# Storing the turned blocks of the first expert table in another order: four stores by groups of 32 partitions instead of four by groups of columns

## Chip, cores and metric

The kernel runs on one core of one Trainium2 chip. The metric is the device time of one execution in microseconds. Three runs of the kernel before are shown with their median.

## What is computed

The reference is one layer of a hybrid encoder on 528 positions (16 learned tokens and 512 of the input) of width 2048, in float32:

```python
h += (sigmoid(g_a) * mlstm_branch(...) + sigmoid(g_b) * conv_branch(...)) @ w_o
h += peer(rmsnorm(h), w_q, sub_keys, expert_u, expert_v)      # 8 heads, top 16 of 128 x 128 experts
# in peer, for each token t and each of its 128 chosen experts e:
z   = einsum('thed,td->the', expert_u[eidx], tb)
act = gates * gelu(z)
out = einsum('the,thed->td', act, expert_v[eidx])
```

`expert_u` and `expert_v` are tables of 16384 rows of 2048 floats (128 MB each).

## The kernel before, in words

**Stages.** All large products go through one stream of weight blocks of 128x2048 floats (1 MB): 48 blocks for the mLSTM heads (6 a head, 8 heads), 64 for the convolution branch and the gates (4 to each of 16 channel tiles), 16 each for the mLSTM output, the convolution output, `w_o` and the query projection, and then 128 for the first expert table and 128 for the second. SP loads a block into one of two buffers `w_raw` (line 393), ScalarE makes its rounded part `w_hi` (line 1047), VectorE the rest `w_lo` (line 1424), and TensorE multiplies three times per block of 128 rows of depth (lines 757 to 759): high by high, high by low, low by high. In the first two stages the blocks have either 2x264 moving columns (96 matmuls) or 512 (48 matmuls).

**Two ways through the expert tables.** 384 of the 512 tokens meet the experts densely: all 16384 products by matmul. The last 128 tokens, one to each partition, gather the rows of their 128 chosen experts one after another with an indirect DMA (`u_row`, line 687, for the first table; line 716 for the second), and VectorE takes the dot product. For that the tables must lie in DRAM by rows. The second is copied from DRAM to DRAM (`row_copy`, line 389, 128 copies of 1 MB in runs of 1 KB). The first lies in blocks `u_blocks[m]` of 128 depths x 2048 and must be turned on the way.

**The turned blocks.** For each block m of 128 SP loads 1 MB into one of two buffers `u_raw` (`u_load`, line 396). VectorE turns it with a transpose of 32x32 squares into one buffer `u_turned` (`u_turn`, lines 1426 to 1432). Before it may write there, all four stores of block m-1 must have landed (`u_stored`, line 1434, four semaphores `ur_st`). Then SP, which waits for the turn (line 400), stores the buffer to `u_rows` with four DMAs (line 402) and issues the load of block m+2 (line 405). One turned row of an expert lies in `u_rows` as four pieces of 512 floats, one from each group `a` of 32 partitions. Each of the four DMAs takes a quarter `b` of the columns of all 128 partitions:

```python
for b in range(QD):                                     # QD = 4
    sp.dma_start(u_rows[m, b, :, :, :].rearrange("r a n -> a r n"),
                 bufs[1][:, b * D // QD:(b + 1) * D // QD]).then_inc(ur_st[b], 16)
```

so that its DRAM side has the shape (4, 32, 512) and its SBUF side (128, 512).

**Order of the work.** It is written out by hand. In SP's program each weight load is followed by the stores of one turned block, the load of a further one and, in part of the stages, one or two row copies. In VectorE's program the turns stand between the `w_lo` of successive blocks and the stage's own work (attention of a head; 31 taps of the convolution, line 1616; the merge and the residual, lines 1727, 1730). The turns are spread so: blocks 0 to 37 over the heads, 38 to 98 over the convolution tiles, 99 to 113 over the convolution output, 114 to 127 over `w_o` and the first query blocks, each set with buffers of its own (names with a, b and c). Except at the seams there is one turn to a weight block. The stage of the mLSTM output has one turned block at its start and two row copies to each weight block.

**Who needs `u_rows`.** GpSimd waits for all stores (line 698) after the routing. VectorE computes the row indices of the gather once, ahead of it (lines 1910 to 1918): `ix_z = 128 j + i`, since the row of expert (i, j) is row `(j b r)` of `u_rows` with i = 32 b + r.

Of the kernel before, what the change touches and what calls it, by code (L numbers as in the profile page):

```python
# [33 lines left out]
F32 = mybir.dt.float32  # L34
F32R = mybir.dt.float32r
U32 = mybir.dt.uint32
ALU = mybir.AluOpType
# [4 lines left out]
P = 128  # L42
D = 2048
KT = D // P
# [7 lines left out]
KEYS = 128  # L52
# [19 lines left out]
VSLOT = 3  # L72
V_FIRST, V_LAST = 1, 119
QD = P // 32
# [15 lines left out]
def encoder_block(nc, xT, w_proj, w_gate, b_gate, w_mo, w_co, w_o, w_q, u_blocks, v_blocks, cols,  # L90
# [5 lines left out]
    z_dram = nc.dram_tensor("z_scratch", (NB_E, P, NT), F32, kind="Internal").ap()  # L96
    g_dram = nc.dram_tensor("g_scratch", (NT // CH, P, KEYS * CH), F32, kind="Internal").ap()
    v_rows = nc.dram_tensor("v_rows", (KEYS // GJ, P, GJ, GJ, 256), F32, kind="Internal").ap()
    u_rows = nc.dram_tensor("u_rows", (KEYS, QD, 32, QD, KT * 32), F32, kind="Internal").ap()

    at = [(nc.sbuf_base + 31) // 32 * 32]

# [118 lines left out]
    GB, UG = [GB0, GB1], [UG0, UG1, UG2]  # L221
# [17 lines left out]
    with ExitStack() as ctx:  # L239
# [5 lines left out]
        def sem(name):  # L245
            return ctx.enter_context(nc.semaphore(name))
# [81 lines left out]
        ur_st = [sem(f"u_rows_stored{b}") for b in range(QD)]  # L328
# [39 lines left out]
        def _(sp):  # L368
# [26 lines left out]
            def u_load(m, bufs):  # L395
                sp.dma_start(bufs[0][m % 2][:, :], u_blocks[m]).then_inc(ur_ld[m % 2], 16)

            def u_turned(m, bufs, end):

                sp.wait_ge(ur_turn, m + 1)  # L400
                for b in range(QD):
                    sp.dma_start(u_rows[m, b, :, :, :].rearrange("r a n -> a r n"), bufs[1][:, b * D // QD:(b + 1) * D // QD]  # L402
                                 ).then_inc(ur_st[b], 16)
                if m + 2 < end:
                    u_load(m + 2, bufs)

            for n in range(2, NB_A1 + NB_A2):
                weights(w_proj, n, A1)
                x = n - 2
                if x == U_A1_X - 1:  # L410
                    sp.wait_ge(x_lo, KT)
                    sp.wait_ge(g_rdy, 1)
                    for v in range(2):
                        u_load(U_A1 + v, u_a1)
                if U_A1_X <= x < U_A1_X + U_A2 - U_A1:
                    u_turned(x - U_A1_X + U_A1, u_a1, U_A2)
                if x == U_A2_X - 1:
                    sp.wait_ge(hs_done, 2 * NH)
                    for v in range(2):
                        u_load(U_A2 + v, u_a2)  # L420
                if U_A2_X <= x:
                    u_turned(x - U_A2_X + U_A2, u_a2, U_B2)
                if n < 8:
                    row_copy(2 * n - 4)
                    row_copy(2 * n - 3)
                elif n < 46:
                    row_copy(n + 4)
                elif n < 52:
                    row_copy(2 * n - 42)
                    row_copy(2 * n - 41)  # L430
                elif n < 54:
                    row_copy(n + 10)
            sp.wait_ge(hs_done, 2 * NH)
            sp.dma_start(sk[:], sub_keys).then_inc(sk_ld, 16)
            for n in range(NB_16):
                weights(w_mo, n, B1)
                x = B1 + n - 2
                if x < U_A2_X + U_B2 - U_A2:
                    u_turned(x - U_A2_X + U_A2, u_a2, U_B2)
                for v in range(2):  # L440
                    row_copy(64 + 2 * n + v)
# [81 lines left out]
        def _(pool):  # L523
# [160 lines left out]

            def u_row(p):

                pool.indirect_dma_start(UG[p % VSLOT][:, :], None, u_rows.rearrange("j b r a n -> (j b r) (a n)"),  # L687
                                        bass.IndirectOffsetOnAxis(ap=ZI[:, p:p + 1], axis=0)).then_inc(ug_ld[p % VSLOT], 16)

            def z_stores(n):  # L690
# [9 lines left out]
            for p in range(VSLOT):  # L700
                u_row(p)
            for n in range(Z_LOOK, NB_E):
                z_stores(n)
                for p in dots(n):
                    if p + VSLOT < P:
                        pool.wait_ge(ug_dot, p + 1)
                        u_row(p + VSLOT)
                if n == Z_LOOK + Z_GATE + 1:
                    for s in range(2):
                        pool.wait_ge(g_st[s], 8 * (NT // CH) + 16)  # L710
                        pool.wait_ge(z_st[s], 8 * (Z_LOOK + Z_GATE))
                    group_load(pool, 0, 0, zg_first, gg_first)
# [678 lines left out]
        def _(dve):  # L1391
# [6 lines left out]
            def step(ins):  # L1398

                ins.then_inc(v_step, 1)  # L1400
                chain["k"] += 1
                return here()

            def link(ins):

                dve.wait_ge(v_step, step(ins))
# [33 lines left out]
            for m2 in range(KT // 2):  # L1440
                a, b = ((sq0, sq1), (sq2, sq3))[m2 % 2]
# [467 lines left out]
            ei, ej = EI[:, TG, :], EJ[:, TG, :]  # L1909
            link(dve.tensor_copy(ixu[:, :], ej))  # L1910
            link(dve.tensor_scalar(ixs[:, :], ixu[:, :], 3, None, ALU.logical_shift_right))
            link(dve.tensor_copy(ixf[:, :], ixs[:, :]))
            link(dve.scalar_tensor_tensor(ixz[:, :], ej, float(P), ei, ALU.mult, ALU.add))
            link(dve.scalar_tensor_tensor(ixf[:, :], ixf[:, :], float(P * GJ - GJ), ej, ALU.mult, ALU.add))
            link(dve.scalar_tensor_tensor(ixf[:, :], ei, float(GJ), ixf[:, :], ALU.mult, ALU.add))
            dve.tensor_copy(ZI[:, :], ixz[:, :]).then_inc(ix_rdy, 1)
            dve.tensor_copy(VI[:, :], ixf[:, :]).then_inc(ix_rdy, 1)
            dve.tensor_copy(GS[:, :], GA[:, TG, :]).then_inc(ix_rdy, 1)
# [13 lines left out]
            with dve.Fori(0, NT // CH // 2) as cc:  # L1932
                for b in range(8):
                    n = 8 * cc + b
# [12 lines left out]
            with dve.Fori(0, 8) as i:  # L1947
                for b in range(6):
                    n = 6 * i + (Z_LOOK + Z_GATE + b)
# [47 lines left out]
            for g in range(KEYS // GJ):  # L1997
                par, more, tail = g % 2, g < KEYS // GJ - 1, g == KEYS // GJ - 1
                for r in range(8):
                    n = 8 * g + r  # L2000
# [95 lines left out]
```

## Time and profile before

| | |
|---|---|
| three runs, median (lowest to highest) | 5224.12 us (5221.38 to 5229.09) |
| the profiled execution, its own time | 5226.97 us |
| its span, first to last instruction | 5225.4 us |
| mean granted TensorE clock | 0.945 of full |
| TensorE matmul busy | 4625.4 us, 89% |
| VectorE busy | 3327.7 us, 64% |
| DMA | 1272.96 MB, mean 244 GB/s |

How to read it: a busy TensorE is not one at its peak, because matmuls are pipelined and their ends are modelled. The granted clock is the share of the full 2.4 GHz that the chip gave in a stretch. The DMA share is the mean busy share of the core's 16 DMA engines. "SPq" is SP's queue, in which DMAs are issued. In the chain of waits and in the table of waits a DMA is named by destination and source, as `u_rows<-u_turned_a`.

### The profile page before, as it was taken

Reading aid. Unit: us, or ns where it says so; the run is one execution under the profiler, and the core shown is the slowest. Engines: PE = TensorE matmul, PEld = TensorE weight load, DVE = VectorE, ACT = ScalarE, POOL = GpSimd, SP = SyncE. Lnnn points to the kernel's source line nnn. Section 1 sums busy time; section 2 is a strip of 40 time slices with the busy share of each in tenths; the row PEclk is TensorE's granted clock in tenths of the full one; section 3 lists DMA queues with packets and bytes.
Section 4 is the critical chain, followed back from the end, with each engine's and each line's share of the span. In section 5 each row is a group of like instructions: output and inputs, shape, how many; then the busy total and the mean of one; then the engine's idle time right before and its main releaser. Section 6 shows DMA issues by size and latency. Waiting matters only on the chain.

```text
span 5225.4 us, 66426 instructions
## 1 busy us (share of the span) xinstructions
PE 4625.4 (89%) x24985; PEld 4220.1 (81%) x24985; DVE 3327.7 (64%) x4044; ACT 1306.1 (25%) x1217; POOL 710.3 (14%) x742
## 2 busy tenths in 40 slices
PE   8988889867777778976769899999999999999998
PEld 6767667766666666865657799999999999999998
DVE  5555456555555565433238978887776578888886
ACT  4222222111111112311121234443222322222223
POOL 1000101000000002000001111222332011111112
PEclk9989999988888888998989999999999999999999
DMA  6666666555555558655567357778888688888884
GB/s 233 240 233 234 233 233 239 196 185 190 179 194 183 193 181 301 226 187 183 205 226 273 125 178 276 287 289 325 339 332 297 240 300 316 308 309 307 313 289 164
DMA packets 383856, 1272.96 MB, mean 244 GB/s; under 512 B 22144, under 2 KB 198160, under 8 KB 276128
## 3 DMA queue, kind: packets, MB, share of 16 engines
q1 hardware_dynamic: 329728, 940.49, 50.5%
q0 software_dynamic: 54048, 331.51, 17.3%
q8 instruction: 37, 0.61, 0.0%
q14 instruction: 43, 0.35, 0.0%
HBM read 1070.46 MB, written 335.61 MB: 269 GB/s over the span
## 4 chain that ended last, share of the span: by engine, by line
PE 47%; DMA 32%; DVE 10%; SPq 6%; issue 3%; ACT 1%; POOL 1%; DVEq 0%; POOLq 0%; ACTq 0%
DMA u_rows<-u_turned_a 23%; PE bank L757 15%; PE bank L758 15%; PE bank L759 15%; SPq L402 5%; DVE u_turned_a L1431 4%; DMA u_rows<-u_turned_b 4%; DMA u_rows<-u_turned_c 3%; PE bank L981 1%; DMA u_raw_a<-u_blocks 1%; DVE w_lo L1424 1%; DVE u_turned_b L1431 1%; POOL cand L674 1%; ACT w_hi L1047 1%; DVE u_turned_c L1431 1%
## 5 line engine op out<-in xcount | busy, mean ns | idle before, releaser
L757 PE MATMUL bank<-x_hi,w_hi 128*128 128x384 f32 (+2 forms) x5760 | 2049.1, 356 | 540.9 <-DVE w_lo L1424 424.5
L758 PE MATMUL bank<-x_lo,w_hi 128*128 128x384 f32 (+2 forms) x5760 | 2029.4, 352 | 0.0
L759 PE MATMUL bank<-x_hi,w_lo 128*128 128x384 f32 (+2 forms) x5760 | 2017.5, 350 | 0.0
L757 PEld LDWEIGHTS bank<-x_hi,w_hi 128*128 128x128 f32 x5760 | 1143.1, 198 | 679.5 <-issue 449.2
L1047 ACT ACTIVATE w_hi<-w_raw 128x2048 fp32r<-128x2048 f32 x432 | 826.8, 1914 | 2177.6 <-PE bank L759 1717.6
L1424 DVE TENSOR_TENSOR w_lo<-w_raw,w_hi 128x2048 fp32r<-128x2048 f32 x432 | 993.7, 2300 | 350.8 <-ACT w_hi L1047 348.9
L759 PEld LDWEIGHTS bank<-x_hi,w_lo 128*128 128x128 f32 x5760 | 1143.0, 198 | 88.0
L758 PEld LDWEIGHTS bank<-x_lo,w_hi 128*128 128x128 f32 x5760 | 1143.8, 199 | 86.3 <-issue 1.2
L1431 DVE STREAM_TRANSPOSE u_turned_a<-u_raw_a 128x2048 f32<-128x2048 f32 x99 | 228.8, 2311 | 767.1 <-DMA u_rows<-u_turned_a 767.1
L757 PE MATMUL bank<-x_hi_o,w_hi 128*128 128x384 f32 x2048 | 684.4, 334 | 0.6 <-DVE w_lo L1424 0.4
L759 PE MATMUL bank<-x_hi_o,w_lo 128*128 128x384 f32 x2048 | 684.1, 334 | 0.0
L758 PE MATMUL bank<-x_lo_o,w_hi 128*128 128x384 f32 x2048 | 684.1, 334 | 0.0
L757 PEld LDWEIGHTS bank<-x_hi_o,w_hi 128*128 128x128 f32 x2048 | 384.5, 188 | 1.2 <-issue 1.2
L758 PEld LDWEIGHTS bank<-x_lo_o,w_hi 128*128 128x128 f32 x2048 | 384.5, 188 | 0.0
L759 PEld LDWEIGHTS bank<-x_hi_o,w_lo 128*128 128x128 f32 x2048 | 384.5, 188 | 0.0
L1990 DVE SCALAR_TENSOR_TENSOR v_sums<-v_row,gate_pairs,v_sums 128x2048 f32<-128x2048 f32 x128 | 300.3, 2346 | 1.0
L1929 DVE SCALAR_TENSOR_TENSOR u_row<-u_row,x_rows 128x2048 f32<-128x2048 f32 x128 | 290.3, 2286 | 0.0
L716 POOL DMA_INDIRECT v_row<-v_rows,v_index x128 | 153.2, 1197 | 836.0 <-DVE v_sums L1990 832.6
L687 POOL DMA_INDIRECT u_row<-u_rows,z_index x128 | 185.8, 1452 | 345.9 <-DVE u_row L1929 333.6
L1616 DVE SCALAR_TENSOR_TENSOR r<-glu,conv_w,r 128x512 f32 (+1 forms) x240 | 178.4, 743 | 0.0
L1616 DVE SCALAR_TENSOR_TENSOR conv_odd<-glu,conv_w,conv_odd 128x512 f32<-128x512 f32 x224 | 166.5, 743 | 0.0
L1845 DVE TENSOR_TENSOR z_stage<-bank,rstd_b 128x384 f32<-128x384 f32 x128 | 71.2, 556 | 148.1 <-PE bank L759 140.0
(280 smaller groups left out, 2689.6 us busy)
## 6 DMA issues: line engine op xcount, KB each, us to landing
v_rows<-v_blocks SPq DMA_DIRECT2D x128, 1024.0 KB, 11.7
w_raw<-u_blocks SPq DMA_DIRECT2D x128, 1024.0 KB, 5.7
w_raw<-v_blocks SPq DMA_DIRECT2D x128, 1024.0 KB, 4.9
w_raw<-w_proj SPq DMA_DIRECT2D x112, 1024.0 KB, 13.7
u_raw_a<-u_blocks SPq DMA_DIRECT2D x99, 1024.0 KB, 13.6
u_rows<-u_turned_a SPq DMA_DIRECT2D x396, 256.0 KB
z_scratch<-z_stage POOLq DMA_DIRECT2D x128, 192.0 KB, 3.4
g_scratch<-g_chunk SPq DMA_DIRECT2D x12, 2048.0 KB, 12.1
```

Of the source, the lines that this page charges most:

```text
L402: sp.dma_start(u_rows[m, b, :, :, :].rearrange("r a n -> a r n"), bufs[1][:, b * D // QD:(b + 1) * D // QD]).then_inc(ur_st[b], 16)
L687: pool.indirect_dma_start(UG[p % VSLOT][:, :], None, u_rows.rearrange("j b r a n -> (j b r) (a n)"), bass.IndirectOffsetOnAxis(ap=ZI[:, p: ...
L716: pool.indirect_dma_start(VG[p % VSLOT][:, :], None, v_rows.rearrange("g i j d c -> (g i j) (d c)"), bass.IndirectOffsetOnAxis(ap=VI[:, p: ...
L757: pe.matmul(dst, whi, xhi, start=start, stop=False)
L758: pe.matmul(dst, whi, xlo, start=False, stop=False)
L759: return pe.matmul(dst, wlo, xhi, start=False, stop=stop)
L1047: act.activation(WH[s][:, :], RAW[s][:, :], ACT.Copy).then_inc(w_hi, 1)
L1424: dve.tensor_tensor(WL[s][:, :], RAW[s][:, :], WH[s][:, :].bitcast(F32), ALU.subtract).then_inc(w_lo, 1)
L1431: dve.transpose(bufs[1][:, :].rearrange("p (b k c) -> p b k c", b=QD, c=32), bufs[0][s][:, :].rearrange("p (k b c) -> p b k c", b=QD, c=32 ...
L1616: at_.append(step(dve.scalar_tensor_tensor(acc, x, w, acc, ALU.mult, ALU.add)))
L1929: dve.scalar_tensor_tensor(UG[s][:, :], UG[s][:, :], 1.0, XR[:, :, :, :].rearrange("p a k c -> p (a k c)"), ALU.mult, ALU.mult, accum_out= ...
L1990: dve.scalar_tensor_tensor(ACC[:, :], VG[p % VSLOT][:, :], GS[:, p:p + 1], ACC[:, :], ALU.mult, ALU.add).then_inc(vg_use, 1)
```

## The change

A block of `u_rows` keeps its size but its order becomes row r, column quarter b, partition group a. Each store now takes all columns of one group of 32 partitions, as 4 runs of 2 KB from each; the DRAM side has the shape (32, 4, 512), the SBUF side (32, 4, 512). The gather's rows are still 8 KB in one piece, and their number becomes `128 j + 4 r + b` = `128 j + 4 i - 127 (i >> 5)`, with four more small instructions on VectorE.

```diff
-    u_rows = nc.dram_tensor("u_rows", (KEYS, QD, 32, QD, KT * 32), F32, kind="Internal").ap()
+    u_rows = nc.dram_tensor("u_rows", (KEYS, 32, QD, QD, KT * 32), F32, kind="Internal").ap()
...
                 sp.wait_ge(ur_turn, m + 1)
-                for b in range(QD):
-                    sp.dma_start(u_rows[m, b, :, :, :].rearrange("r a n -> a r n"), bufs[1][:, b * D // QD:(b + 1) * D // QD]
-                                 ).then_inc(ur_st[b], 16)
+                for a in range(QD):
+                    sp.dma_start(u_rows[m, :, :, a, :], bufs[1][32 * a:32 * a + 32, :].rearrange("r (b n) -> r b n", b=QD)
+                                 ).then_inc(ur_st[a], 16)
...
-                pool.indirect_dma_start(UG[p % VSLOT][:, :], None, u_rows.rearrange("j b r a n -> (j b r) (a n)"),
+                pool.indirect_dma_start(UG[p % VSLOT][:, :], None, u_rows.rearrange("j r b a n -> (j r b) (a n)"),
...
-            link(dve.scalar_tensor_tensor(ixz[:, :], ej, float(P), ei, ALU.mult, ALU.add))
+            link(dve.tensor_scalar(ixz[:, :], ei, float(QD), None, ALU.mult))
+            link(dve.scalar_tensor_tensor(ixz[:, :], ej, float(P), ixz[:, :], ALU.mult, ALU.add))
             link(dve.scalar_tensor_tensor(ixf[:, :], ixf[:, :], float(P * GJ - GJ), ej, ALU.mult, ALU.add))
             link(dve.scalar_tensor_tensor(ixf[:, :], ei, float(GJ), ixf[:, :], ALU.mult, ALU.add))
+            link(dve.tensor_copy(ixu[:, :], ei))
+            link(dve.tensor_scalar(ixs[:, :], ixu[:, :], 5, None, ALU.logical_shift_right))
+            link(dve.scalar_tensor_tensor(ixz[:, :], ixs[:, :], 1.0 - 32 * QD, ixz[:, :], ALU.mult, ALU.add))
```

## Rows read from the trace of the kernel before

**Rows 1.** The page, parts 1 and 2: busy shares, and 40 slices of the span.

```profile
PE 4625.4 (89%) x24985; PEld 4220.1 (81%) x24985; DVE 3327.7 (64%) x4044; ACT 1306.1 (25%) x1217; POOL 710.3 (14%) x742
...
PEclk9989999988888888998989999999999999999999
...
GB/s 233 240 233 234 233 233 239 196 185 190 179 194 183 193 181 301 226 187 183 205 226 273 125 178 276 287 289 325 339 332 297 240 300 316 308 309 307 313 289 164
```

**Rows 2.** The page, part 4: the chain that ended last, by line.

```profile
DMA u_rows<-u_turned_a 23%; PE bank L757 15%; PE bank L758 15%; PE bank L759 15%; SPq L402 5%; DVE u_turned_a L1431 4%; DMA u_rows<-u_turned_b 4%; DMA u_rows<-u_turned_c 3%; PE bank L981 1%; DMA u_raw_a<-u_blocks 1%; DVE w_lo L1424 1%; DVE u_turned_b L1431 1%; POOL cand L674 1%; ACT w_hi L1047 1%; DVE u_turned_c L1431 1%
```

**Rows 3.** The table of waits, whole span: us in total, times, longest us.

```profile
DVE u_turned_a L1431 <- DMA u_rows<-u_turned_a: 767.1, 90, 14.3
...
ACT w_hi L1047 <- DMA w_raw<-w_proj: 248.5, 37, 16.3
...
DVE u_turned_b L1431 <- DMA u_rows<-u_turned_b: 150.7, 13, 13.0
...
DVE u_turned_c L1431 <- DMA u_rows<-u_turned_c: 138.0, 13, 13.5
...
ACT w_hi L1047 <- DMA w_raw<-w_co: 113.2, 7, 16.8
```

**Rows 4.** The chain in order of time, one cycle: start us, us, what.

```profile
2251.83 2.32 DVE u_turned_b L1431
...
2254.17 0.51 SPq L402
...
2255.27 0.72 SPq L402
...
2256.04 14.16 DMA u_rows<-u_turned_b
```

**Rows 5.** Line 1431 in three stretches: duration ns min/median/max, first and last start us.

```profile
L1431 DVE STREAM_TRANSPOSE u_turned_a<-u_raw_a x18: 2302/2311/2316, 457.0 to 774.5; 128x2048 f32<-128x2048 f32 x18
...
L1431 DVE STREAM_TRANSPOSE u_turned_a<-u_raw_a x55: 2311/2311/2316, 1001.6 to 1952.0; 128x2048 f32<-128x2048 f32 x55
...
L1431 DVE STREAM_TRANSPOSE u_turned_b<-u_raw_b x11: 2311/2312/2316, 2233.8 to 2415.7; 128x2048 f32<-128x2048 f32 x11
```

**Rows 6.** Windows: length, PE, PEld, DVE, ACT, POOL busy, clock, DMA share, GB/s.

```profile
2264.00:2268.00 4.00, 4.00 (x19) 3.23 (x18) 0.00 (x0) 0.00 (x0) 0.00 (x0) 1.00 1.00 416
2270.00:2272.00 2.00, 0.00 (x0) 0.00 (x0) 1.68 (x1) 0.00 (x0) 0.00 (x0) 0.88 0.25 107
2288.00:2290.00 2.00, 2.00 (x10) 1.50 (x8) 0.90 (x1) 0.00 (x0) 0.00 (x0) 1.00 0.25 105
```

**Rows 7.** The page, part 6: count, KB each, median us from issue to landing.

```profile
z_scratch<-z_stage POOLq DMA_DIRECT2D x128, 192.0 KB, 3.4
...
out<-h_rows SPq DMA_DIRECT2D x1, 1024.0 KB, 5.5
```

**Rows 8.** Line 1913, a small VectorE instruction of the index arithmetic.

```profile
L1913 DVE SCALAR_TENSOR_TENSOR ix_z<-ej,ei x1: 291/291/291, 3098.0 to 3098.0; 128x128 f32<-128x128 f32 x1
```

**Rows 9.** Line 1424 ahead of the turns of the convolution output.

```profile
L1424 DVE TENSOR_TENSOR w_lo<-w_raw,w_hi x5: 2281/2292/2293, 2182.5 to 2225.6; 128x2048 fp32r<-128x2048 f32 x5
```

**Rows 10.** Windows: heads, convolution, mLSTM output, convolution output, and two of 6 us.

```profile
450.00:774.00 324.00, 270.39 (x1446) 223.09 (x1444) 172.32 (x152) 69.50 (x73) 29.74 (x57) 0.92 0.67 237
1001.60:1952.00 950.40, 702.22 (x3903) 631.93 (x3902) 537.71 (x573) 129.98 (x108) 57.38 (x40) 0.86 0.53 186
2007.70:2160.00 152.30, 152.30 (x656) 122.84 (x655) 77.62 (x82) 50.84 (x49) 34.64 (x33) 1.00 0.89 310
2237.00:2419.00 182.00, 137.43 (x519) 107.38 (x517) 58.61 (x41) 27.96 (x24) 5.43 (x11) 0.88 0.53 188
...
1001.00:1007.00 6.00, 6.00 (x52) 6.00 (x51) 5.41 (x6) 0.00 (x0) 0.00 (x0) 1.00 0.24 80
2184.00:2190.00 6.00, 6.00 (x27) 4.87 (x26) 0.77 (x1) 0.00 (x0) 0.00 (x0) 1.00 0.69 221
```

**Rows 11.** The chain at the start of the query blocks.

```profile
2716.65 24.77 DMA u_rows<-u_turned_c
```

## The prediction

> **What bounds the kernel now.** I read the page's busy shares and slices first. TensorE is busy 89% of the span, but the granted clock falls to the eighties (in per cent) in the ninth to sixteenth slice and the DMA rate to 179 to 196 GB/s there [rows 1]: in the first half neither TensorE nor DMA is full. The chain of waits says why: 30% of the span is the landing of `u_rows` stores, 5% their issue on SP (line 402) and some 5% the transposes between them [rows 2]. The table of waits has the same thing on VectorE: 767 + 151 + 138 = 1056 us of waiting at line 1431 for earlier stores of the turned block, 116 times [rows 3]. One buffer holds the turned block, so block m+1 can't be turned before the four stores of block m have landed; and since VectorE works in order, the `w_lo` that TensorE needs stands behind that wait.
>
> The chain row by row shows the loop: turn 2.32, issue of the stores 1.87 (2254.17 to 2256.04), landing of the last 14.16, together 18.5 us from turn to turn [rows 4]. So one turn costs L + 4.3, L being the time from the last issue to landing. By the turns of line 1431 the cycle is (774.5-457.0)/17 = 18.7 us in the heads, (1952.0-1001.6)/54 = 17.6 in the convolution stage, (2415.7-2233.8)/10 = 18.2 in the output projection [rows 5].
>
> **Why the landing takes so long.** While stores and loads run together all 16 DMA engines are busy: share 1.00, 416 GB/s. But around the end of two cycles the share is 0.25, at 107 and 105 GB/s [rows 6]: a quarter of the engines still work at their full rate while the rest have nothing. I read this as each store running on 4 engines, one for each of the 4 entries of its outermost DRAM dimension `(a, r, n)`. These 4 carry 256 KB of the block's store and 64 KB of each of the two 1 MB loads, 384 KB in all at 26.7 GB/s: 14.7 us. That is the landing. The queue is in the engines: the stores of [rows 4] have landed by 2270.2, and from 2270 to 2272 the share is 0.25 still, so what runs there are the loads' parts that stood behind them.
>
> **The change, part by part.**
> 1. The stores. Still four of 256 KB and 128 runs of 2 KB, but with 32 outermost on both sides (32 partitions; 32 DRAM rows). The loads, with 128 outermost on both sides, keep all engines busy, so by the reading above the new stores spread over 16. A block's work per engine is then (1 + 1 + 1 MB)/16 = 192 KB, 7.6 us at 416 GB/s over all, in place of 14.7 on four. Bounds for the new L: 192 KB from 128 partitions land in 3.4 us, 1 MB in 5.5 [rows 7]; above, today's 14.2. Four stores behind one another are 1 MB, and a weight load may be ahead of them, so I take L = 7 (5.5 and 1.5 for sharing). The loop then needs 7 + 4.3 = 11.3 us a turn. Nothing is excluded below, but it would buy little, as TensorE comes next. How many engines the new shape gets, no row shows. The Trainium skill, "DMA: Bandwidth & Descriptors", the section on why a semaphore rises by 16, gives the count as the largest number up to 16 that divides the slowest dimension of both sides: 4 now, with which the share of 0.25 agrees, and 16 afterwards; by it rival D below is out and the sum stands.
> 2. Issues on SP: four of 0.5 us before and after [rows 4]. The stores pass no other queue entry. Cost zero; the cover is SP's idle time, and if a store's issue grew by 0.1 us, the loop would grow by 0.4.
> 3. The gather of `u_row` reads rows of 8 KB in the same number; only the index differs. Zero.
> 4. Four more small VectorE instructions on 128x128 at the end of routing: one such takes 0.29 us [rows 8], so 1.2 us at most with nothing beside them; I count 1 whole.
>
> **What is late next, stage by stage.**
> - Output projection and `w_o` stage. Before the turns start the same blocks follow each other in (2225.6-2182.5)/4 = 10.8 us [rows 9]; that is TensorE's time (27 matmuls in 6 us, full clock [rows 10]). The loop's 11.3 is beside it, through one VectorE queue: I take 12. 25 cycles x (18.2 - 12) = 155; the four turns at the seams, one of which waits 24.8 us for a landing [rows 11], another 10.
> - Convolution, tiles of 4 blocks and 4 turns, 70.4 us now. TensorE: 52 matmuls in 6 us [rows 10], so a gate-linear block of 96 takes 11.4 or less, one of 48 wide matmuls 10.8: 44.4 a tile. VectorE is busy 537.7 of 950.4 us, 39.8 a tile. The loop needs 4 x 11.3 = 45.2. Three things near 45 that wait for one another: I take 48.5. 15 tiles x (70.4 - 48.5) = 328.
> - Heads, 6 blocks, 6 turns, 112 us now (18.7 x 6). TensorE is busy 270.4 of 324 us at a granted clock of 0.92 [rows 10]: 93.5 a head, and 8% of the stretch (9 a head) at most is what the clock took, so between 84.6 and 93.5 is TensorE's floor. I take 89.5. 6 heads x 22.5 = 134.
> - DMA in sum: share 0.67, 0.53 and 0.53 of those stretches [rows 10] is 75 us a head, 37 a tile, 9.6 a turn. That fits under the new times at shares of 0.84, 0.77 and 0.80; and before the output projection there is a stretch with TensorE busy without a gap, at clock 1.00, while DMA stands at 0.89 and 310 GB/s [rows 10], so this much traffic alone doesn't starve it. `w_raw` landings, for which ScalarE waits 249 + 113 us [rows 3], fall with the same cause and are not counted again.
> - The later half holds no such store (the chain has none) and isn't touched.
>
> Sum: 155 + 10 + 328 + 134 - 1 = 626. The profiled execution took 5226.97 us (span 5225.4), 2.9 above the median of the three runs, 5224.12. 5227 - 626 = 4601; against the median 4598. I say **4600**.
>
> **Rivals.**
> *B: the stores are spread but run at half the rate, since each now reads one group of 32 partitions.* For: no row shows a large transfer from 32 partitions, all fast ones have 128. Then 1 MB takes 5.0 us of all engines rather than 2.5, and since later loads queue behind it, DMA time per block grows by 2.5: 75 + 15 = 90 a head, 37 + 10 = 47 a tile, 12.1 a turn, which at the best share seen with TensorE full, 0.89, is 101, 53 and 13.6 us. Gains 6 x 11 + 15 x 17.4 + 25 x 4.6 = 442: **4785**. The Trainium skill, "SBUF — State Buffer", section on the DMA port swizzle, speaks against the change here: 32 partitions reach 8 of 16 ports, with 189 GB/s measured for 1 MiB; an estimate from it is 5.5 us for the four stores where B has 5.0, by which B would be some 50 us slower and my forecast would be B. No row here shows it.
> *C, the slow side: a group of 32 partitions gives only the 107 GB/s that today's store gets.* The trace can't tell whether a quarter of the engines or the quarter of the partitions that each of them reads is the limit. If it is the partitions, 1 MB still takes 9.8 us, but now it blocks all 16 engines and every load behind it: +7.3 us of DMA time a block. (75 + 44)/0.89 = 134 a head, (37 + 29)/0.89 = 74 a tile, 16.9/0.89 = 19.0 a turn: +22 x 6, +4 x 15, +1 x 25, **5440**. Against it: the tail after the stores' landing [rows 6] lies in the engines; and loads at 416 GB/s put 104 into each such group at once, so the ceiling of a group would have to lie just there. It decides below about 120 GB/s for one store.
> *D: the stores still use 4 engines*, for example because the DRAM side (rows 4 apart, merged) is split as before. Then L stays: **5228**.
> *E: the loop falls to L = 4.* Then only TensorE's floors are left: 86.5 a head, 45.5 a tile, 11 a turn: 6 x 25.5 + 15 x 25 + 25 x 7.2 + 10 = 718, **4510**.
>
> **Chances.** Forecast 0.52, B 0.22, E 0.16, C 0.06, D 0.04. The forecast's own ends, L 5.5 to 8.5, heads 87 to 93, give 4540 to 4670. The range takes E and B in, B with a little over its price: 4500 to 4830; C and D and the tails are what is left out. About 0.2% (10 us) is what a measurement can tell here. Forecast, B and E are faster: 0.90; D is the same: 0.04; C slower: 0.06.
>
> **What would show each step.** The landing of `u_rows` in the chain at 5 to 8 us in place of 14, its waits on VectorE from 1056 to under 250 us, and no stretch at a share of 0.25. Turns of line 1431 about 15, 12 and 12 us apart in the three stages. Granted clock in the convolution stage near 1.0, the rate 230 to 300 GB/s. The lengths after the last turn (the expert stages, some 2480 us) unchanged within 5. For B: share near 1.0 in stretches where the rate is about 220 GB/s. For C: the same at about 107. For D: 0.25 again. I would be wrong in the step on TensorE's floors if the turns no longer waited and the cycle were still over 13 us in the output projection.

## The result and the profile after

The changed kernel takes 4530.05 us (median of 4 runs, 4528.72 to 4531.28) against 5224.64 us for the kernel before (4 runs): a ratio of 0.867, 95% interval 0.8655 to 0.8685. The forecast was 4600 with a range of 4500 to 4830; the kernel got 695 us faster where some 625 were forecast. The profiled execution took 4528.72 us, its span is 4527.2.

The page of the changed kernel, parts 1 and 2, answers to [rows 1]:

```profile
PE 4451.7 (98%) x24985; PEld 4089.4 (90%) x24985; DVE 3336.6 (74%) x4048; ACT 1301.7 (29%) x1217; POOL 712.1 (16%) x742
...
PEclk9999999999999999999999999999999999999999
...
GB/s 214 320 288 291 314 280 229 288 286 290 286 289 287 332 229 286 286 322 311 151 141 238 294 287 281 308 354 332 332 262 238 314 319 293 315 316 301 307 290 149
```

The stretch of slices at 179 to 196 GB/s with the clock in the eighties is gone: most slices of the first half stand at 280 to 320 GB/s, and the clock is at nine tenths or more in every slice. TensorE went from 89% to 98% of a shorter span. Part 4 of the same page, the chain by line, answers to [rows 2]:

```profile
PE bank L757 26%; PE bank L758 26%; PE bank L759 26%; DMA u_rows<-u_turned_b 2%; PE bank L981 2%; DMA u_rows<-u_turned_c 1%; SPq L402 1%; DVE w_lo L1424 1%; PE bank L857 1%; DVE u_turned_b L1431 1%; PE bank L864 1%; ACT w_hi L1047 1%; DVE u_turned_c L1431 1%; PE bank L833 1%; POOL cand L674 1%
```

30% of a longer chain was the landing of stores; it is 3% now. The table of waits of the changed kernel (us in total, times, longest) answers to [rows 3]:

```profile
DVE u_turned_a L1431 <- DMA u_rows<-u_turned_a: 43.0, 34, 4.8
```

And its line 402, with who waited for the stores (us, times) and their landings:

```profile
  DVE u_turned_c L1431: 4.4, 1
  DVE u_turned_b L1431: 3.4, 1
...
DMA to landing us min/median/max: 3.0/5.7/13.0
```

1056 us of waiting at line 1431 became 51. ScalarE's waits of 249 and 113 us for `w_raw` from `w_proj` and `w_co` are no longer among the 60 longest (the last of them is 11.5 us). The 5.7 us is the median over all stores. What compares with the 14.16 us of [rows 4], last issue to landing, is the chain in order of time (start us, us, what), one cycle of the output projection:

```profile
1718.34 2.32 DVE u_turned_b L1431
...
1721.91 0.74 SPq L402
1722.69 5.75 DMA u_rows<-u_turned_b
```

Over the cycles of that stage this last landing takes 5.1 to 6.3 us. The stores have no fewer bytes, runs or issues than before.

The pace in the three stages. Lines 1424 and 1431 of the changed kernel, with first and last start: the last head, the convolution, the output projection (the last answers to the third line of [rows 5]):

```profile
L1424 DVE TENSOR_TENSOR w_lo<-w_raw,w_hi x7: 2291/2293/2294, 644.4 to 732.2; 128x2048 fp32r<-128x2048 f32 x7
...
L1424 DVE TENSOR_TENSOR w_lo<-w_raw,w_hi x37: 2284/2293/2295, 1007.0 to 1417.7; 128x2048 fp32r<-128x2048 f32 x37
...
L1431 DVE STREAM_TRANSPOSE u_turned_b<-u_raw_b x11: 2302/2304/2306, 1718.3 to 1829.5; 128x2048 f32<-128x2048 f32 x11
```

A head takes 87.8 us (112 before), a tile of four blocks 4 x 410.7/36 = 45.6 (70.4 before), a block of the output projection 11.1 (18.2 before). Windows over the same stages (length, PE, PEld, DVE, ACT, POOL busy, clock, DMA share, GB/s) answer to [rows 10]:

```profile
320.00:640.00 320.00, 320.00 (x1855) 265.52 (x1854) 218.17 (x191) 87.48 (x92) 42.94 (x75) 1.00 0.88 297
838.40:1431.60 593.20, 593.20 (x3746) 538.48 (x3745) 514.00 (x547) 124.30 (x104) 54.05 (x39) 1.00 0.88 288
...
1718.30:1829.50 111.20, 111.20 (x482) 90.15 (x481) 59.57 (x41) 19.20 (x10) 5.37 (x10) 1.00 0.93 307
```

In each of them TensorE is busy without a gap at full clock. The bound has moved to it, with DMA not far behind at shares of 0.88 to 0.93. The loop of the turns is not far behind either: turn and issue 4.4, landing about 5.6, so some 10 of the 11.1 us of a block in the output projection. Behind the last turn nothing changed. One window of each kernel, from the last turn to the end:

```profile
2741.50:5225.40 2483.90, 2424.67 (x13912) 2384.85 (x13912) 1916.72 (x2671) 758.79 (x675) 483.64 (x443) 0.99 0.76 277
```

```profile
2042.40:4527.20 2484.80, 2434.83 (x13964) 2393.49 (x13962) 1917.33 (x2676) 761.11 (x677) 481.50 (x443) 0.99 0.76 278
```

The difference is 0.9 us, which is what the four new index instructions can account for (0.23, 0.23, 0.23 and 0.29 us by their rows).

### The profile page after: what moved, and what is told of

The parts are those of the page before. It is cut to its first block, busy times and chain, and to the rows that moved or that the text cites. A ratio compares the mean times of both kernels' runs of the same rounds, so it can differ in the third digit from the quotient of the medians.

```text
span 4527.2 us, 66430 instructions
## 1 busy us (share of the span) xinstructions
PE 4451.7 (98%) x24985; PEld 4089.4 (90%) x24985; DVE 3336.6 (74%) x4048; ACT 1301.7 (29%) x1217; POOL 712.1 (16%) x742
## 4 chain that ended last, share of the span: by engine, by line
PE 83%; DVE 6%; DMA 5%; issue 3%; SPq 2%; ACT 1%; POOL 1%; DVEq 0%; POOLq 0%; ACTq 0%
PE bank L757 26%; PE bank L758 26%; PE bank L759 26%; DMA u_rows<-u_turned_b 2%; PE bank L981 2%; DMA u_rows<-u_turned_c 1%; SPq L402 1%; DVE w_lo L1424 1%; PE bank L857 1%; DVE u_turned_b L1431 1%; PE bank L864 1%; ACT w_hi L1047 1%; DVE u_turned_c L1431 1%; PE bank L833 1%; POOL cand L674 1%
## 5 line engine op out<-in xcount | busy, mean ns | idle before, releaser
L757 PE MATMUL bank<-x_hi,w_hi 128*128 128x384 f32 (+2 forms) x5760 | 1973.5, 343 | 27.0 <-DVE w_lo L1424 19.7
L758 PE MATMUL bank<-x_lo,w_hi 128*128 128x384 f32 (+2 forms) x5760 | 1966.6, 341 | 0.0
L759 PE MATMUL bank<-x_hi,w_lo 128*128 128x384 f32 (+2 forms) x5760 | 1958.0, 340 | 0.0
L757 PEld LDWEIGHTS bank<-x_hi,w_hi 128*128 128x128 f32 x5760 | 1084.6, 188 | 131.9 <-issue 39.2
L759 PEld LDWEIGHTS bank<-x_hi,w_lo 128*128 128x128 f32 x5760 | 1087.6, 189 | 82.4
L758 PEld LDWEIGHTS bank<-x_lo,w_hi 128*128 128x128 f32 x5760 | 1085.2, 188 | 84.7 <-issue 2.6
L2009 DVE TENSOR_TENSOR out_sums<-bank,out_sums 128x384 f32<-128x384 f32 x256 | 130.5, 551 | 52.2 <-PE bank L759 48.0
## 6 DMA issues: line engine op xcount, KB each, us to landing
g_scratch<-g_chunk SPq DMA_DIRECT2D x12, 2048.0 KB, 12.1
```

Source lines behind the costliest of these rows:

```text
L757: pe.matmul(dst, whi, xhi, start=start, stop=False)
L758: pe.matmul(dst, whi, xlo, start=False, stop=False)
L759: return pe.matmul(dst, wlo, xhi, start=False, stop=stop)
L2009: dve.tensor_tensor(o, o_bank[r % 2][k][:, 0:NT], o, ALU.add).then_inc(evac_v, 1)
```

## The experiments

The theory: each store ran on only 4 of the 16 DMA engines, because the outermost dimension of its DRAM side was 4; with 32 outermost on both sides it runs on all 16, and that is the whole effect. Rivals: the order of the pieces in DRAM does it; or the choice of partitions; or the wait on the single turned buffer, whatever the engines do.

### Order of rows and cut of the stores, one at a time

The change has two halves that need not go together. The first kernel keeps the old order of rows and the old index arithmetic:

```diff
-                for b in range(QD):
-                    sp.dma_start(u_rows[m, b, :, :, :].rearrange("r a n -> a r n"), bufs[1][:, b * D // QD:(b + 1) * D // QD]
-                                 ).then_inc(ur_st[b], 16)
+                for a in range(QD):
+                    sp.dma_start(u_rows[m, :, :, a, :].rearrange("b r n -> r b n"), bufs[1][32 * a:32 * a + 32, :].rearrange("r (b n) -> r b n", b=QD)
+                                 ).then_inc(ur_st[a], 16)
```

> The kernel before, with its own order of rows in DRAM and its own index arithmetic, and only the four stores cut as in the changed kernel: one for each group of 32 partitions, both sides (32, 4, 512). Theory (the number of DMA engines that a store runs on is the whole effect, and it comes from the outermost dimension, 32 instead of 4): as the changed kernel within 0.2%, 4530 us, perhaps 1 us less since the four index instructions are gone; landings of u_rows at 5.7 us. Rival (the new order of the pieces in DRAM is what makes the stores fast): back towards 5225 us, landings near 14 us.

Measured: 4531.14 us, ratio to before 0.8672 (0.8658 to 0.8686); landings 5.7 us, as in the changed kernel. The second keeps the new order and cuts by columns:

```diff
-                for a in range(QD):
-                    sp.dma_start(u_rows[m, :, :, a, :], bufs[1][32 * a:32 * a + 32, :].rearrange("r (b n) -> r b n", b=QD)
-                                 ).then_inc(ur_st[a], 16)
+                for b in range(QD):
+                    sp.dma_start(u_rows[m, :, b, :, :].rearrange("r a n -> a r n"), bufs[1][:, b * D // QD:(b + 1) * D // QD]
+                                 ).then_inc(ur_st[b], 16)
```

> The changed kernel with its new order of rows and its index arithmetic, but the stores cut by columns as before: 128 partitions, DRAM side (4, 32, 512). Theory (engines): as the kernel before, 5225 us within 0.5%, landings of 13 to 14 us, stretches with a DMA share of 0.25. Rival (order in DRAM): 4530 us.

Measured: 5222.89 us, ratio 0.9995 (0.9983 to 1.0008). Its table of waits and a window at the end of a cycle are those of the kernel before:

```profile
DVE u_turned_a L1431 <- DMA u_rows<-u_turned_a: 771.5, 90, 14.8
```

```profile
2252.00:2254.00 2.00, 2.00 (x10) 1.65 (x9) 0.00 (x0) 0.00 (x0) 0.00 (x0) 1.00 0.26 99
```

What follows: the new order of rows in DRAM does nothing for the time, either way, and isn't needed. The cut of the stores is all of it.

### The same stores on 2, 8 and 16 engines

The cut changes two things at once: the outermost dimension and the partitions that a store reads. These three kernels leave the stores as they were (128 partitions, a quarter of the columns, 128 runs of 2 KB into the same 256 KB of DRAM) and change only the order of the pieces, so that the outermost dimension of the DRAM side is `k`. The rows that are gathered later are then mixed from several experts, in the same number and size. The number `k` stands for 8, 16 and 2:

```diff
-                    sp.dma_start(u_rows[m, b, :, :, :].rearrange("r a n -> a r n"), bufs[1][:, b * D // QD:(b + 1) * D // QD]
-                                 ).then_inc(ur_st[b], 16)
+                    sp.dma_start(u_rows[m, b, :, :, :].rearrange("r a n -> (r a) n").rearrange("(r a) n -> a r n", a=k),
+                                 bufs[1][:, b * D // QD:(b + 1) * D // QD]).then_inc(ur_st[b], 16)
```

k = 8:

> The kernel before with the same four stores of 128 partitions, but the pieces of each go to DRAM in an order with 8 outermost, (8, 16, 512); the rows that the last 128 tokens gather are thereby mixed from several experts. Theory: 8 engines carry 128 KB of store and 2 x 64 KB of loads a block, 256 KB at 26.7 GB/s = 9.6 us, which is under TensorE's 11.1: nearly the whole gain, 4530 to 4600 us, landings of 7 to 9 us, and stretches with a DMA share near 0.5. A theory in which only a change of partition groups or of the DRAM order helps has no reason for a value between; it gives 5225 or 4530.

k = 16:

> The same with 16 outermost, (16, 8, 512): every store runs on all engines and reads all 128 partitions; the gathered rows are mixed. Theory engines: 4529 us, as the changed kernel. It tells rival B of the prediction (a group of 32 partitions slows a store): if that costs anything, landings here are shorter than the 5.7 us of the changed kernel, by about 2.5 us if the rate is halved there; if it costs nothing, they are 5.7 too.

k = 2:

> The kernel before with the pieces of each store in an order with 2 outermost, (2, 64, 512); gathered rows mixed. Theory engines: the two carry 512 KB of store and 2 x 64 KB of loads a block, 640 KB at 26.7 GB/s = 24.5 us; landings of about 24 us and turns 28 us apart where there are no row copies, so 128 turns x 10 us more than before: 6500 us (6100 if the store of one block and the loads of the next overlap better than now). DMA share of 0.125 in some stretches. If engines were not the limit, 5225.

Measured (with the kernel before as k = 4; turns are those of the output projection; each ratio is to executions of the kernel before that ran beside it; k = 2 and k = 8 were run twice each):

| outermost dimension | time, us | ratio to before (95%) | turns apart, us | waits at line 1431, us |
|---|---|---|---|---|
| 2 | 6403.22 | 1.227 (1.2249 to 1.2298) | 26.8 | 2203 |
| 4 | 5224.64 | 1 | 18.2 | 1056 |
| 8 | 4608.05 | 0.882 (0.8798 to 0.8841) | 11.8 | 319 |
| 16 | 4530.17 | 0.867 (0.8654 to 0.8688) | 11.1 | 12 |

How many engines ran can be counted. The line on packets of the page, for k = 2, 4, 8 and 16 in this order (the last is the same in the changed kernel):

```profile
DMA packets 382832, 1272.96 MB, mean 199 GB/s; under 512 B 21120, under 2 KB 197136, under 8 KB 275104
```

```profile
DMA packets 383856, 1272.96 MB, mean 244 GB/s; under 512 B 22144, under 2 KB 198160, under 8 KB 276128
```

```profile
DMA packets 385904, 1272.97 MB, mean 276 GB/s; under 512 B 24192, under 2 KB 200208, under 8 KB 278176
```

```profile
DMA packets 390000, 1272.99 MB, mean 281 GB/s; under 512 B 28288, under 2 KB 204304, under 8 KB 282272
```

The packets under 512 B number 20096 + 512 k to the last one. There are 512 stores and the data is the same, so I read it as one small packet for each engine that a store runs on. So the outermost dimension is the number of engines, for 2, 4, 8 and 16, as the Trainium skill ("DMA: Bandwidth & Descriptors", on why a semaphore rises by 16) has it. Windows of the kernel with two engines show the share that goes with it, an eighth of 16, at half the rate that four engines gave:

```profile
3248.00:3252.00 4.00, 4.00 (x12) 3.09 (x11) 0.00 (x0) 0.00 (x0) 0.00 (x0) 0.59 0.13 51
3252.00:3256.00 4.00, 4.00 (x19) 3.25 (x18) 0.00 (x0) 0.00 (x0) 0.00 (x0) 1.00 0.13 51
```

k = 16 came out as expected. For k = 2, 6500 us and turns 28 us apart were expected where 6403 and 26.8 came. The expectation for k = 8, up to 4600, was too low by 8 us. It counted bytes (256 KB on each of eight engines, 9.6 us) and left out that a turn still has to wait for its landing: turns there are 11.8 us apart in the output projection and (2072.6 - 1940.0)/10 = 13.3 in the `w_o` stage, where TensorE would allow 11.1:

```profile
L1431 DVE STREAM_TRANSPOSE u_turned_c<-u_raw_c x11: 2305/2312/2315, 1940.0 to 2072.6; 128x2048 f32<-128x2048 f32 x11
```

### Do 32 partitions slow a store?

Rival B of the prediction. The kernel with k = 16 reads all 128 partitions in each store and differs from the changed kernel in that. Its landings are 4.4 us in the median where the changed kernel has 5.7, so 1.3 us shorter and not the 2.5 that a halved rate would give; in the output projection alone it is 5.4 against 5.5. The time is the same. Two more, both from the changed kernel: all four stores read partitions 0 to 31 (so three quarters of each turned block are left out), or the groups are taken in another order.

```diff
                 for a in range(QD):
-                    sp.dma_start(u_rows[m, :, :, a, :], bufs[1][32 * a:32 * a + 32, :].rearrange("r (b n) -> r b n", b=QD)
+                    sp.dma_start(u_rows[m, :, :, a, :], bufs[1][0:32, :].rearrange("r (b n) -> r b n", b=QD)
```

> The changed kernel, with all four stores reading partitions 0 to 31 (the rows in DRAM are thereby a quarter repeated four times). Theory engines alone: nothing changes, 4530 us, landings 5.7. If a group of 32 partitions has a ceiling (rival B), the four stores can no longer share out over the groups: landings of 7 us or more and a rate of about 220 GB/s at a DMA share near 1 during the stores; the total stays within 20 us of 4530 since TensorE is busy without a gap and DMA has some 10% left.

```diff
-                for a in range(QD):
+                for a in (0, 2, 1, 3):
```

> The changed kernel with the four stores issued in the order of groups 0, 2, 1, 3, so that neighbours in the queue read different halves of the 128 partitions. Theory engines alone: 4530 us, landings 5.7. If groups 0 and 1, and 2 and 3, share one ceiling, neighbouring stores overlap better: landings 0.5 to 1.5 us shorter. The total is the same either way, within 0.2%.

Measured: 4532.15 us (ratio 0.8686, 0.8672 to 0.8701) with landings of 5.5, and 4530.08 us (0.8685, 0.867 to 0.8699) with landings of 5.4. The cost shows in the DMA share of the same stretch of the convolution stage at the same rate. k = 16 with 128 partitions, the changed kernel, one group four times:

```profile
850.00:1420.00 570.00, 570.00 (x3633) 519.08 (x3632) 491.31 (x524) 119.36 (x100) 53.02 (x37) 1.00 0.84 287
```

```profile
850.00:1420.00 570.00, 570.00 (x3625) 518.65 (x3624) 492.45 (x523) 119.32 (x100) 52.95 (x37) 1.00 0.88 287
```

```profile
850.00:1420.00 570.00, 570.00 (x3632) 519.00 (x3631) 492.33 (x523) 119.32 (x100) 52.95 (x37) 1.00 0.93 287
```

A block takes 11.4 us there, so the stores of one block cost the engines 0.04 x 11.4 = 0.5 us more from groups than from all partitions, and 1.0 us when it is always the same group. (The shares are rounded to 0.01, which is 0.1 us. The order in DRAM is not the cause: the kernel with groups and the old order has 0.88 as well.) The packet records in the traces give a little less: the 2 KB packets, nearly all of them the stores', took 98.8, 106.3 and 121.9 ns in the mean in these three kernels, and 32 of them for each engine and block make 0.2 and 0.7 us more. So what the Trainium skill ("SBUF — State Buffer", section on the DMA port swizzle) leads one to expect, a cost of using few partitions, is there, at a fifth or less of the 2.5 us that rival B counted. The median landing did not rise to 7 us. With the groups in the order 0, 2, 1, 3 the share is 0.87 and the median landing 0.3 us shorter, in the output projection 0.6 longer: no clear difference. In a stretch of the changed kernel in which, by the order of issue, mostly stores run, the rate is well over half of the 416 GB/s of [rows 6], which rival B counted. In the kernel that reads one group four times, a stretch behind the issue of the stores does come near the 220 GB/s at a share near 1 that was given as B's sign (277 in the kernel with k = 16 at the same distance from its issue). It is short, and the mean cost over a block stays at the 0.7 to 1.0 us above. The changed kernel first, then that one:

```profile
1745.00:1748.00 3.00, 3.00 (x15) 2.43 (x14) 0.26 (x1) 0.41 (x1) 0.00 (x0) 1.00 0.91 324
```

```profile
1749.00:1752.00 3.00, 3.00 (x15) 2.43 (x14) 1.44 (x2) 1.79 (x1) 0.04 (x1) 1.00 0.97 229
```

### Is it the wait or the engines?

One could also have given the turned block a second buffer and left the stores on four engines. In the `w_o` stage there is room for one (14 of the 128 blocks). The parts of the edit that matter:

```diff
+    u_c1 = (u_c1[0], [u_c1[1], place("u_turned_c1b", [P, D], F32, r2 + 12 * row)])
...
+                src, done = (bufs[1][m % 2], ur2[m % 2]) if bufs is u_c1 else (bufs[1], ur_st)
...
+                if bufs is u_c1:
+                    for b in range(QD):
+                        dve.wait_ge(ur2[s][b], 16 * n - 16 * (U_C1 // 2 - 1))
```

> The kernel before, stores on four engines, but in the w_o stage (blocks 114 to 127) the turned block has two buffers, each with store semaphores of its own, so that a turn waits for the stores of the block before last only. It tells the loop (turn, issue, landing, turn) from the throughput of the four engines. Theory of the prediction (384 KB on each of four engines a block at 26.7 GB/s): turns there move from 18.1 us apart to the engines' 14.7, 15 us with the seams; the kernel gains about 10 x 3.2 us, 5190 us. Rival (the wait on the single buffer is all, the engines keep up): turns 11.1 us apart, at TensorE's pace, 5150 us. If nothing but the landing of the loads sets the pace, 18.1 stays.

Measured: 5200.08 us, ratio 0.9954 (0.9943 to 0.9966). Turns in that stage (line 1442 in this kernel), and what they now wait for, in a window of eight of them:

```profile
L1442 DVE STREAM_TRANSPOSE u_turned_c<-u_raw_c x4: 2311/2312/2315, 2541.1 to 2635.9; 128x2048 f32<-128x2048 f32 x4
L1442 DVE STREAM_TRANSPOSE u_turned_c1b<-u_raw_c x4: 2311/2311/2315, 2556.6 to 2651.4; 128x2048 f32<-128x2048 f32 x4
...
  DMA u_raw_c<-u_blocks: 63.6, 8
```

They are (2651.4 - 2541.1)/7 = 15.8 us apart: not 18.1, and not TensorE's 11.1. Expected were 15 us and 5190 in all. The wait has moved from the stores to the load of the next block. I read this as the throughput of the four engines, in whose queues a quarter of each load stands behind the stores (14.7 us by the prediction's bytes, which leave out side traffic). What speaks for it is the rate in 40 slices of the `w_o` stage, first the kernel before (2508 to 2671 us), then this one (2520 to 2680):

```profile
GB/s 107 125 193 390 111 92 147 402 161 71 122 282 305 102 105 123 402 169 67 125 275 315 97 106 164 412 117 66 127 303 290 98 109 179 404 117 50 134 321 271
```

```profile
GB/s 217 103 187 415 155 100 229 418 109 101 205 422 128 103 219 420 119 99 252 395 108 103 284 363 108 101 289 358 112 99 294 357 108 101 329 272 296 284 101 221
```

Before, the rate falls to between 50 and 71 GB/s in four slices, well under the 107 that four busy engines give; here no slice is under 99. But SP is held up too: the issue of the four stores took 13.0, 12.9 and 8.9 us in three cycles in a row, where it takes 1.9 in [rows 4], and the load stands behind it in SP's program. No run separates a late issue from a long queue. So before the change the loop (18.1) stood only a little above what the same four engines allowed with a second buffer (15.8), and of the two ways only more engines brought 11.1.

## Why the prediction was right, and where a size was off

- **The bound and its mechanism.** Right. The loop of turn, issue, landing, turn was what the first half hung on, and the quarter share in [rows 6] was indeed 4 of 16 engines, which the count of small packets confirms. The sentence that the queue lies in the engines and not in the partitions is borne out by the kernel with 128 partitions and 16 engines. The forecast's number was less good than its mechanism: 4530 lies below the forecast's own ends (4540 to 4670), and inside the range only because that took in E. What came about is E's state, with only TensorE's floors left, which had a chance of 0.16.
- **L.** Forecast 7, measured 5.7 in the median and 5.1 to 6.3 on the chain, near the 5.5 of the 1 MB store in [rows 7] without the 1.5 added for sharing. Lowering it further brings nothing: the kernel with k = 16 has 12 us of waits in place of 51 and the same time.
- **The terms.** The taps of the convolution, line 1616, divide the span (before, then after):

```profile
L1616 DVE SCALAR_TENSOR_TENSOR r<-glu,conv_w,r x240: 708/746/752, 916.6 to 2022.9; 128x512 f32 x105, 128x512 f32<-128x512 f32 x15
```

```profile
L1616 DVE SCALAR_TENSOR_TENSOR r<-glu,conv_w,r x240: 708/747/755, 781.9 to 1512.8; 128x512 f32 x105, 128x512 f32<-128x512 f32 x15
```

Up to the first tap, which is the heads, 134.7 us were saved (forecast 134); from there to the last 375.4 (328); after it 188.1 (164). That is the 698 us between the spans. By cycles the convolution is 15 x (70.4 - 45.6) = 372 and the output projection with `w_o` 25 x (18.2 - 11.1) = 177, index arithmetic costs 1, which leaves 12 for the seams (10 forecast). For the heads 6 x (112.1 - 87.8) would be 146, 11 more than were saved. So six heads at these paces are too many, and the forecast's 134 was right partly by luck: it took a pace of 89.5 that was too slow, on the same six.
- **What was mis-sized** is L, and with it the allowances for a loop of 11.3 us beside TensorE: 48.5 a tile where 45.6 came, 44 us in all, and 12 where 11.1 came, 22 us. For an L of 7 the allowances were good, as far as the kernel with k = 8, whose engines are also fuller, can stand for it. There the last landings on the chain take 6.2 to 8.6 us in the output projection and in the convolution from 990 to 1300 us. Its turns are 11.8 us apart in the first and (1485.1 - 855.1)/52 = 12.1 in the second, which is 48.5 a tile, and it takes 4608 us in all:

```profile
L1431 DVE STREAM_TRANSPOSE u_turned_a<-u_raw_a x53: 2303/2311/2314, 855.1 to 1485.1; 128x2048 f32<-128x2048 f32 x53
```

In the changed kernel the loop takes about 10 us, 40 a tile, VectorE is busy 514.00/13 = 39.5 a tile, and TensorE 593.20 of 593.20 us: with the loop a tenth under TensorE's pace, nothing is added to it. TensorE's own floor had been put at 44.4 a tile and is 45.6. Why the remaining waits of 51 us cost nothing was not tested; I take it that the two weight blocks TensorE has in hand cover them.
- **The rivals.** B was priced by halving the rate of the stores, 2.5 us a block; measured is 0.5 or less. C is ruled out by the kernel that reads one group four times and takes 4532 us, D by the packets. E came nearest with 4510: its floors, 86.5, 45.5 and 11, are close to the measured 87.8, 45.6 and 11.1, though L = 4 was not needed for them.
- **DMA.** Forecast shares of 0.84, 0.77 and 0.80, measured 0.88, 0.88 and 0.93: the stages are shorter than forecast, and the engine time a block is up by about 0.7 us (0.93 x 11.1 = 10.3 a turn of the output projection against 9.6). By these shares DMA is the next bound; no run tests that.
- **Slips.** The prediction puts the rate of 179 to 196 GB/s in the ninth to sixteenth slice; it is in the eighth to fifteenth, and the sixteenth has 301. And 6 x 22.5 is 135, not 134. Neither bears on the result.

## What to carry to other kernels

When many transfers land late although the DMA engines are far from busy, look for stretches with a DMA share of a whole number of sixteenths. Here a store whose DRAM side had an outermost dimension of 2, 4, 8 or 16 ran on just that many engines, and it held up every load that has a part in their queues: the 1 MB loads of `u_raw_a` landed after 13.6 us in the median before and after 8.3 with the change. The stretch has to come back in each cycle. A single one proves nothing: the kernel with k = 16 has a microsecond at 0.26 and 107 GB/s too. Cut such a transfer so that the outermost dimension of both sides is a multiple of 16 (measured here: 16 and 32 on the DRAM side, 128 and 32 on the other); neither the bytes nor the number of issues need change, nor the layout in DRAM. A second buffer hides only the wait: with four engines it brought 18.1 down to 15.8 us a block, where 16 engines brought 11.1. And once a loop is a tenth below the bound, a shorter landing brings nothing more.

## What was not expected of the hardware

Four stores in a row of 32 partitions each cost the engines at most 0.5 us a block more than stores of 128 partitions, and at most 1.0 when all read the same 32, of some 10 us in all. The Trainium skill, "SBUF — State Buffer", gives 189 GB/s for one 1 MiB transfer with 32 partitions; no run here had one store in flight by itself, so none contradicts that figure, but with several stores and loads in the queues the rate was 324 GB/s over the 3 us shown above, and 229 in the other stretch, with stores from one and the same group. And DMA at a share of 0.93 and 307 GB/s left no gap in TensorE, while a mean share of 0.53 had left it idle a quarter of the time: the mean over the engines says nothing of the four that are full.
